# Differential attention of a hybrid layer: a packed stationary block for the sample rows, a shorter softmax merge, and squares on ScalarE

## The reference, cut to what matters

```python
z = h @ w_in                                   # q1|q2, k1|k2, v of a head are 3 x 128 of its columns
q, k = rope_partial(q), rope_partial(k)        # first quarter of each 64-wide half
s = einsum('bqhmd,bkhmd->bhmqk', q, k) * 64**-0.5   # two maps m per head, chunk-causal mask
p = softmax(s)
a = p[:, :, 0] - lam * p[:, :, 1]
attn = a @ v
attn = rms_norm(attn, subln_g) * (1 - lam_init)     # per row and head, over 128 values
```

## Time and profile before

| | |
|---|---|
| median of 3 runs | 946.29 us (943.45 to 947.93) |
| the profiled execution's own time | 945.17 us |
| its span | 943.2 us |
| mean granted TensorE clock | 0.96 of 2.4 GHz |
| busy: PE, PEld, DVE, ACT, POOL | 851.2, 750.7, 603.1, 505.3, 107.6 us |

### The profile page before, as it was taken

One profiled execution on the slowest core, in us unless ns is written; L12 is line 12 of the kernel. 1 busy time (PEld: TensorE's weight loads), 2 busy tenths in 40 slices (PEclk: granted clock), 3 DMA queues, 4 the chain that ended last, 5 costly groups with the idle time before them and its releaser, 6 DMA issues.

```text
span 943.2 us, 15744 instructions
## 1 busy us (share of the span) xinstructions
PE 851.2 (90%) x5052; PEld 750.7 (80%) x5052; DVE 603.1 (64%) x1047; ACT 505.3 (54%) x907; POOL 107.6 (11%) x115
## 2 busy tenths in 40 slices
PE   4998999999999999899899998189999999999980
PEld 4998999888888889889898787167777778777760
DVE  6264224676676676566555311658989998998892
ACT  6235213554544544354623212158878887887883
POOL 0000000000000000000000001202432342233221
PEclk8999999999999999999999998579999999999995
DMA  8622133033033023041322914779999999999975
GB/s 247 153 90 65 51 90 84 14 97 96 0 96 96 24 78 97 9 153 43 112 77 82 353 47 158 234 229 315 330 318 333 343 333 346 345 329 327 342 258 202
DMA packets 156131, 164.99 MB, mean 175 GB/s; under 512 B 20877, under 2 KB 140301, under 8 KB 156090
## 3 DMA queue, kind: packets, MB, share of 16 engines
q1 hardware_dynamic: 149706, 152.69, 49.9%
q0 software_dynamic: 6096, 11.17, 4.4%
q10 hardware_dynamic: 288, 0.59, 0.2%
HBM read 153.71 MB, written 19.60 MB: 184 GB/s over the span
## 4 chain that ended last, share of the span: by engine, by line
PE 74%; DVE 8%; DMA 6%; ACT 5%; issue 4%; SPq 2%; ACTq 0%; POOL 0%; DVEq 0%; POOLq 0%
PE ps L1355 23%; PE ps L1357 21%; PE ps L1356 21%; DMA rawM<-in_w_expert_up 2%; PE ps L1494 2%; ACT E L760 2%; SPq L470 2%; PE ps L1663 1%; PE ps L1503 1%; DMA xg<-h_rows,idn 1%; PE ps L1616 1%; DVE wl L951 1%; PE ps L1475 1%; ACT wh L724 1%; DMA gb<-in_norm_mix_g 1%
## 5 line engine op out<-in xcount | busy, mean ns | idle before, releaser
L1298 DVE TENSOR_TENSOR wl<-rawM,wh 128x1024 fp32r<-128x1024 f32 x192 | 227.3, 1221 | 24.2 <-ACT wh L873 23.8
L873 ACT ACTIVATE wh<-rawM 128x1024 fp32r<-128x1024 f32 x195 | 199.2, 1055 | 12.0 <-PE ps L1357 7.9
L1355 PE MATMUL ps<-hTh,wh 128*128 128x272 f32 x448 | 132.6, 296 | 8.1 <-ACT plh L712 3.0
L1357 PE MATMUL ps<-hTh,wl 128*128 128x272 f32 x448 | 131.2, 293 | 0.0
L1356 PE MATMUL ps<-hTl,wh 128*128 128x272 f32 x448 | 130.4, 291 | 0.0
L1355 PE MATMUL ps<-wh,hTh 128*128 128x384 f32 x320 | 116.4, 364 | 8.4 <-ACT qkv L737 6.8
L1355 PE MATMUL ps<-wh,xh 128*128 128x512 f32 x256 | 105.0, 410 | 4.5 <-DVE xl L1321 3.6
L1357 PE MATMUL ps<-wh,hTl 128*128 128x384 f32 x320 | 108.1, 338 | 0.0
L1356 PE MATMUL ps<-wl,hTh 128*128 128x384 f32 x320 | 107.8, 337 | 0.0
L1357 PE MATMUL ps<-wh,xl 128*128 128x512 f32 x256 | 101.9, 398 | 0.0
L1356 PE MATMUL ps<-wl,xh 128*128 128x512 f32 x256 | 101.8, 398 | 0.0
(11 more groups left out here) (255 smaller groups left out, 1679.7 us busy)
## 6 DMA issues: line engine op xcount, KB each, us to landing
rawM<-in_w_expert_gate SPq DMA_DIRECT2D x131, 256.0 KB, 5.9
rawM<-in_w_expert_up SPq DMA_DIRECT2D x131, 256.0 KB, 8.3
rawM<-in_w_expert_down SPq DMA_DIRECT2D x64, 512.0 KB, 9.1
rawA<-in_w_in SPq DMA_DIRECT2D x64, 192.0 KB, 3.0
rawA<-in_w_in SPq DMA_DIRECT2D x20, 512.0 KB, 5.1
rawA<-in_w_attn_branch SPq DMA_DIRECT2D x8, 512.0 KB, 4.5
rawA<-in_w_out SPq DMA_DIRECT2D x8, 512.0 KB, 4.2
x<-in_x_prompt SPq DMA_DIRECT2D x4, 512.0 KB, 6.8
```

The costliest lines, as they stand in the source:

```text
L873: nc.scalar.activation(wh[:, c % S, :], rawM[:, slot, :], ACT.Copy).then_inc(m_hi, 1)
L1298: V.tensor_tensor(wl[:, c % S, :], rawM[:, slot, :], wh[:, c % S, :].bitcast(F32), ALU.subtract).then_inc(m_lo, 1)
L1355: T.matmul(out, sh, mh_, start=start, stop=False, **kw)
L1357: return T.matmul(out, sl, mh_, start=False, stop=stop, **kw)
```

## The change

It has these parts. (a) The projection of tile 4 takes a stationary block of 128 columns out of a new tile `dec`, which holds for each j the low parts of the 32 sample rows in columns 64 to 95 and their high parts in 96 to 127 of its window; the first 64 columns of the window are the block before, or zeros. Two matmuls (by `wh`, by `wl`) then give the low rows' products in rows 64 to 95 and the high rows' in 96 to 127 of the bank. (b) `join_sample` on VectorE adds rows 64 to 95 to rows 96 to 127 in `qkv`; the next head's tile 4, `rope` and ScalarE's high part of v wait for it. (c) Map one is no longer scaled; map two is scaled by `esum1 * (1/esum2) * (-lambda)` (`ratio`) and added in one pass, and the row's factor 1/`esum1` is applied by the ScalarE copy into `att`. Map one's exponent gets an addend log(2^-9). (d) The clamp is one operation over tiles 0 to 2 and one over tiles 3 and 4 of a head; squares are ScalarE's alone, a head later, out of `clamped`; VectorE's squares and five of the eight last small operations go.

```diff
 # ScalarE
@@ rows_hi
+                if t == 4:
+                    nc.scalar.activation(dec_hi.rearrange("p (b k) n -> p b k n", b=2), v, ACT.Copy)
+            def square(g, t):
+                act.wait_ge(cl_done, 2 * g + (1 if t < 3 else 2))
+                nc.scalar.activation(clamped[:, t, :], clamped[:, t, :], ACT.Square, scale=SQ_SCALE,
+                                     accum_out=ssb[:, t, bass.ds(g, 1)]).then_inc(sq_done, 1)
             def step(g, s):
+                if s < NT and not (isinstance(g, int) and g == 0):
+                    square(g - 1, s)
                 if s >= 2:
                     act.wait_ge(av_mm, NT * g + s - 1)
-                    nc.scalar.activation(bsq[:], ps[:, 7, 0:P], ACT.Square, scale=BIG_SCALE,
-                                         accum_out=ssb[:, s - 2, bass.ds(g, 1)])
-                    nc.scalar.activation(att[:, s - 2, g, :], ps[:, 7, 0:P], ACT.Copy).then_inc(av_ev, 1)
+                    nc.scalar.activation(att[:, s - 2, g, :], ps[:, 7, 0:P], ACT.Copy,
+                                         scale=rinv[:, s % 2, 0:1]).then_inc(av_ev, 1)
@@ attend
                 act.wait_ge(ckv_in, 32 * (g + 1))
+                act.wait_ge(dec_done, g + 1)
@@ after the last head
             step(HEADS - 1, NT)
+            for t in range(3):
+                square(HEADS - 1, t)
             step(HEADS - 1, NT + 1)
             gate_block(5)
+            for t in range(3, NT):
+                square(HEADS - 1, t)
             warm(ACT.Sqrt)
 # VectorE
@@ rows_lo, t == 4
+                    V.tensor_tensor(dec_lo.rearrange("p (b k) n -> p b k n", b=2), v, oh, ALU.subtract)
+            def clamp(g, part, lk):
+                tiles = slice(0, 3) if part == 0 else slice(3, NT)
+                dve.wait_ge(av_ev, NT * g + (3 if part == 0 else NT))
+                dve.wait_ge(sq_done, NT * (g + 1))
+                V.tensor_scalar(clamped[:, tiles, :], att[:, tiles, g, :], CLAMP, -CLAMP, ALU.min,
+                                ALU.max).then_inc(cl_done, 1)
@@ step(g, s, lk, join=None)
                     lk(V.reciprocal(rinv[:, t % 2, :], esum[:, t % 2, :]))
-                    V.tensor_tensor(rinv[:, t % 2, 1:2], rinv[:, t % 2, 1:2], nlam[:], ALU.mult)
                     a0, a1 = E[t % 2][:, 0, 0:n], E[t % 2][:, 1, 0:n]
-                    lk(V.tensor_scalar(a0, a0, rinv[:, t % 2, 0:1], None, ALU.mult))
-                    V.scalar_tensor_tensor(out=a0, in0=a1, scalar=rinv[:, t % 2, 1:2], in1=a0,
+                    lk(V.scalar_tensor_tensor(out=ratio[:, t % 2:t % 2 + 1], in0=esum[:, t % 2, 0:1],
+                                              scalar=rinv[:, t % 2, 1:2], in1=nlam[:], op0=ALU.mult, op1=ALU.mult))
+                    V.scalar_tensor_tensor(out=a0, in0=a1, scalar=ratio[:, t % 2:t % 2 + 1], in1=a0,
                                            op0=ALU.mult, op1=ALU.add).then_inc(am_done, 1)
+                if join is not None:
+                    join_sample(join)
@@ the same step, after atl
-                if s >= 2:
-                    dve.wait_ge(av_ev, NT * g + s - 1)
-                    lk(V.tensor_scalar(asq[:], att[:, s - 2, g, :], CLAMP, -CLAMP, ALU.min, ALU.max))
-                    ins = V.scalar_tensor_tensor(out=asq[:], in0=asq[:], scalar=1.0,
-                                                 in1=asq[:], op0=ALU.mult, op1=ALU.mult,
-                                                 accum_out=ssa[:, s - 2, bass.ds(g, 1)])
-                    lk(ins)
+                if s == NT:
+                    clamp(g, 0, lk)
+            def join_sample(g):
+                dve.wait_ge(acc_ev, NT * (g + 1))
+                V.tensor_tensor(qkv[LAST:P, 4, :], ps[2 * DEC:LAST, 4, 0:384], qkv[LAST:P, 4, :],
+                                ALU.add).then_inc(dec_done, 1)
@@ attend
                 nxt(3)
+                if not (isinstance(g, int) and g == 0):
+                    clamp(g - 1, 1, lk)
                 nxt(4)
@@ head
-                if not first:
-                    step(h - 2, NT, lk)
+                if first:
+                    join_sample(h - 1)
+                else:
+                    step(h - 2, NT, lk, h - 1)
                 rope(h - 1, lk)
-                if not first:
-                    step(h - 2, NT + 1, lk)
 # TensorE, project
                             pe.wait_ge(acc_ev, NT * (h - 1) + t + 1)
+                            if t == 4:
+                                pe.wait_ge(dec_done, h)
+                    if t < 4:
+                        ins = three(ps[:, t, 0:384], hTh[:, j, col(t)], hTl[:, j, col(t)], wh[:, sl, wc], wl[:, sl, wc],
+                                    j == 0, j == KD - 1)
+                    else:
+                        both = dec[:, 2 * DEC * j:2 * DEC * j + P]
+                        T.matmul(ps[:, t, 0:384], both, wh[:, sl, wc], start=j == 0, stop=False)
+                        ins = T.matmul(ps[:, t, 0:384], both, wl[:, sl, wc], start=False, stop=j == KD - 1)
```

More of the change, by code:

```diff
@@ L148, in build @@
         rinv = small("rinv", [P, 2, 2])
-        ssa = small("ssa", [P, NT, HEADS])
         rsa = small("rsa", [P, NT, HEADS])
         ssb = small("ssb", [P, NT, HEADS])
+        shift = small("shift", [P, 2])
+        ratio = small("ratio", [P, 2])
         wgt = small("wgt", [P, NT, 2])
@@ L825, in _ @@
             step(HEADS - 1, NT)
+            for t in range(3):
+                square(HEADS - 1, t)
             step(HEADS - 1, NT + 1)
             gate_block(5)
+            for t in range(3, NT):
+                square(HEADS - 1, t)
             warm(ACT.Sqrt)
             act.wait_ge(ms_done, 1)
-            nc.scalar.activation(rsa[:], rsa[:], ACT.Sqrt).then_inc(rt_done, 1)
+            nc.scalar.activation(rsa[:], rsa[:], ACT.Sqrt, scale=1.0 / P).then_inc(rt_done, 1)
             split_to(AB0 + 1)
@@ L962, in _ @@
             V.memset(U[:, :, 0:BUF], 0.0).then_inc(pad_done, 1)
+            V.memset(shift[:, 0:1], math.log(MAP_SCALE))
+            V.memset(shift[:, 1:2], 0.0)
+            V.memset(dec[:, 0:2 * DEC].bitcast(F32), 0.0)
             V.memset(idi[:, ROWS:ROWS + 2], 0)
@@ L1059, in lo_head, with step @@
                                 ALU.subtract).then_inc(lo_done, 1)
-            per_head = 1 + 6 * NT
-            per_tail = 6
-            def step(g, s, lk):
+            per_head = 1 + 4 * NT
+            per_tail = 2
+            def clamp(g, part, lk):
[4 more added lines that the diff above has]
+                                ALU.max).then_inc(cl_done, 1)
+            def step(g, s, lk, join=None):
                 if 1 <= s <= NT:
@@ L1081, in step @@
                     lk(V.tensor_reduce(mx[:, s % 2, :], ps[:, 5:7, 0:n], AX.X, ALU.max))
-                    V.tensor_scalar(nb[:, s % 2, :], mx[:, s % 2, :], -SCALE, None, ALU.mult).then_inc(nb_done, 1)
+                    V.scalar_tensor_tensor(out=nb[:, s % 2, :], in0=mx[:, s % 2, :], scalar=-SCALE, in1=shift[:],
+                                           op0=ALU.mult, op1=ALU.add).then_inc(nb_done, 1)
                 if 1 <= s <= NT:
@@ L1156, in _ @@
             split[0] = GB0 + 3
-            step(HEADS - 2, NT, link)
+            step(HEADS - 2, NT, link, HEADS - 1)
             rope(HEADS - 1, link)
-            step(HEADS - 2, NT + 1, link)
             attend(HEADS - 1, lambda k: split_to({3: GB0 + 3, 4: GB0 + 5, 5: GB0 + 7, 6: 0}[k]), link)
             step(HEADS - 1, NT, link)
[L1162 to L1171, removed]
-            link(V.tensor_scalar(fin[:], fin[:], -1.0, 1.0, ALU.mult, ALU.add))
-            link(V.tensor_tensor(rsa[:], rsa[:], fin[:], ALU.mult))
-            link(V.tensor_tensor(rsa[:], rsa[:], isb[:], ALU.add))
-            V.tensor_scalar(fin[:], ssb[:], one, 2.0 ** -20, ALU.is_lt, ALU.mult).then_inc(ms_done, 1)
+            clamp(HEADS - 1, 1, link)
+            full = 2.0 ** 128 * SQ_SCALE ** 2
+            dve.wait_ge(sq_done, NT * (HEADS + 1))
+            link(V.tensor_scalar(rsa[:], ssb[:], full, 1.0 / SQ_SCALE, ALU.min, ALU.mult))
+            V.tensor_scalar(fin[:], ssb[:], full, 2.0 ** -20, ALU.is_lt, ALU.mult)
+            V.tensor_scalar(rsa[:], rsa[:], P * EPS * SQ_SCALE, None, ALU.add).then_inc(ms_done, 1)
             dve.wait_ge(rt_done, NT + 1)
```

19 lines of the change are left out of this document (10 added, 9 removed).

## The result

The changed kernel takes 940.05 us (median of 11 executions, 937.55 to 941.95) and the one before 945.56 in the same runs: ratio 0.9939, 95% interval 0.9928 to 0.9951. The forecast was 939.8 us, with a gain of 6.5 us; the medians differ by 5.5. The profiled execution took 940.75 us with a span of 938.9.

The account below looks back on a forecast made before the run. The kernel looks bound by TensorE, but at five waits chains over other engines end last. Priced by segment, the terms sum to -6.5 us, from 946.3 to 939.8 us (own range 937.5 to 942; full range 934.8 to 945).

Parts of the forecast that it names:

- Head 0 and start of head 1: Head 0's projection and head 1 up to `turn`, where TensorE alone counts: -1.4 and -0.35 us.
- Projection to `turn`: Next head's projection start to the transposes of q and k: -0.6 us in each of six heads, -3.6 in all.
- it had 0.28 to wait: Before the transposes of q and k: TensorE saves 0.35, waited 0.28, so could be ready 0.63 us earlier.
- `turn` to scores 0: Transposes of q and k to scores 0: scaled copy into `att` adds 0.05 us, six times, +0.3.
- Scores 0 to 1: VectorE's chain before scores 1: clamp between two low parts of weights adds 0.28 us, seven times, +2.0.
- Scores 1 to scores 2: Segment with no wait of TensorE: one matmul less, -0.18 us, seven times, -1.2.
- scores 2 to map 2: Scores 2 to map 2's transposes: scale pass goes, `ratio` costs some 0.17; -0.28 us, eight times, -2.2.
- The rest of a head: Map 2's transposes to the next projection: 0 gained, bank wait from 1.11 to about 1.3 us; join covered, no cost.
- The gross: Rival: TensorE's waits are slack and all 11.3 us of removed matmuls count, giving 935.0 us; chance 0.12.
- The eaten gain: Rival: added VectorE clamps run at 0.29 us per tile and eat the gain, 942.5 to 945 us; chance 0.24.
- The clock: Rival: longer TensorE waits bring the clock to 0.50 once a head in six heads, +12, 951.8 us; chance 0.03.
- The join: Rival: the join ends 1.5 + 0.7 us later than placed and lengthens a head, 942 to 947 us; chance 0.05.

Follow-up runs that it names:

- e3: The changed kernel with map one scaled in a pass of its own again and att copied without a scale; ratio to before 0.9946, period 33.55 us.
- e4: The kernel before with late squares on ScalarE and grouped clamps only; ratio to before 1.0008, period 34.06 us.
- e5: The changed kernel with the clamp of tiles 3 and 4 moved to after step 0; ratio to before 0.9934, period 33.07 us.
- e1: The changed kernel with tile 4 projected by three matmuls again, without packing and join; ratio to before 0.9985, period 33.80 us.
- e2: The kernel before with packing and join and nothing else; ratio to before 0.9935, periods 33.57 to 33.66 us.
- e9: The changed kernel with e5, e7, e8 and the clamp cut of e6 together; 925.04 us median, ratio to before 0.9787, period 31.82 us.
- e6: The changed kernel with the clamps cut 4 tiles + 1 instead of 3 + 2; single execution of 939.7 us, period 33.23 us.
- e10: The changed kernel with a gap of 8 elements behind each 128 in `clamped`; single execution of 938.3 us, period 33.30 us.
- e7: The changed kernel with ScalarE emptying banks 0 and 1 before the high part of weight part 6; ratio to before 0.9895, period 32.72 us.
- e8: The changed kernel with VectorE's low part of weight part 5 made after step 3, not step 2; ratio to before 0.9875, period 32.52 us.

## Why the prediction was right, step by step

*Head 0 and start of head 1.* Forecast -1.4 - 0.35 = -1.75; from head 0's first matmul to `turn` of head 0 it was 26.30 before and 24.53 after: -1.77. Head 0's projection alone took 19.65 us for 21.06, where 19.6 for 21.0 was forecast.

*Projection to `turn`.* Forecast -0.60, measured -0.50. The step that failed is "it had 0.28 to wait": that is the idle time of the weight loads, which run ahead of the matmuls and so wait longer (before map 2 they wait 0.54 in the kernel before, the matmuls 0.22). The rows could have told: the five waits add up to 2.24 us, but TensorE's matmuls leave only 34.10 - 32.74 = 1.36 of a head idle, nearly all of it the 0.22 and the 1.11. The matmul of `turn` stood 292.48 - 292.18 = 0.30 behind the one before it, where 0.177 is the plain distance, so TensorE lost 0.12; this and the two removed matmuls, 0.35, give the 0.5 measured. The clamp was mis-sized as well (0.35 forecast and 0.30 from start to start; 0.54 and 0.46 measured), and it cost nothing, since `rope` still ended first.

*`turn` to scores 0.* Forecast +0.05 with bounds 0 and +0.15, measured -0.04, outside them. The copy with its scale does take 0.37 us for 0.27, as weighed, but the segment is no longer for it: e3, whose copy has no scale, has 3.98 as the changed kernel has. The gain came with the late squares, for e4 with these alone has 3.97 for 4.02.

*Scores 0 to 1.* Forecast +0.28, measured +0.20: the clamp lasts 0.28 but the next instruction starts 0.20 after its start. e5 takes exactly that away. The weight loads' wait there grew from 0.35 to 0.73, where about 0.8 was forecast.

*Scores 1 to scores 2, scores 2 to map 2.* Forecast -0.18 and -0.28, measured -0.18 and -0.27. e1, e2, e3 and e4 show which part each belongs to. Before map 2 the matmuls waited 0.22; now 0.13 is left (to 272.15 from the end of the one before, 271.68 + 0.34), under 0.3 as forecast. The weight loads wait 0.46 there, but 0.27 in e1, which has the merge and no packing: the packed blocks bring TensorE earlier. So where work of the same engine ahead of a wait gets shorter, the wait that remains says nothing about the segment. The weight loads in the changed kernel, then in e1:

```profile
272.14 0.31 PEld L1541 LDWEIGHTS ps<-cst,E 128*128 128x128 f32 x3 [0.46 <-DVE E L1104]
```
```profile
275.53 0.31 PEld L1518 LDWEIGHTS ps<-cst,E 128*128 128x128 f32 x3 [0.27 <-DVE E L1098]
```

*The rest of a head.* Forecast 0, measured -0.01 and 0; the wait for the bank is 1.3 as forecast, and the join takes 0.56 and ends over 1 us ahead of its use.

*Sum.* From head 0's first matmul to the first one of the output's projection (454.05) it is 323.84 us for 330.99: -7.15, where -6.5 was forecast; a head gave -0.80 for -0.73. That the head comes out so close is in part luck: over the six heads the segment up to `turn` gave 0.6 us less than forecast, while the two that were to get longer cost 1.1 less. What the medians show is 5.5. The forecast of 939.8 lies within 0.3 of the measured 940.05 because its base, 946.3, was 0.7 above the median of the eleven and its gain 1.0 above the 5.5. The stretch behind that matmul was 482.35 us in the profile before and 484.85 in the one after, 2.5 more (and head 0 begins 0.35 later), and this is over the 2 us that the prediction named as its own refutation outside the heads. The ten experiments, whose code there is the same, have 481.75 (e4) to 485.43 (e1) in their profiles, e9 482.33, without relation to what was gained ahead. So I take it for a scatter between executions, not for an effect. The clock is a part of it: 35 executions of the kernel before, run beside the experiments, took 944.0 us on average where the mean granted clock was 0.963 or 0.964 (12 of them) and 947.6 where it was 0.957 or 0.958 (6). And it can be seen in the traces: behind TensorE's wait of 2.81 us in front of that matmul the clock falls to 0.50 (1.2 GHz) in both kernels, but at another moment. Before, then after:

```profile
462.00:465.00 3.00, 3.00 (x16) 3.00 (x16) 1.06 (x1) 2.99 (x6) 0.00 (x0) 0.55 0.61 189
465.00:468.00 3.00, 3.00 (x24) 3.00 (x23) 0.00 (x0) 2.32 (x4) 0.00 (x0) 0.88 0.83 271
```
```profile
452.00:455.00 3.00, 0.95 (x4) 0.95 (x5) 3.00 (x4) 2.98 (x4) 0.00 (x0) 0.72 0.00 0
455.00:458.00 3.00, 3.00 (x15) 3.00 (x15) 1.27 (x2) 2.99 (x6) 0.00 (x0) 0.50 0.50 170
458.00:461.00 3.00, 3.00 (x18) 3.00 (x17) 0.00 (x0) 2.52 (x4) 0.00 (x0) 0.64 0.78 259
```

By the clock's share that is 3 x 0.45 + 3 x 0.12 = 1.7 us lost before and 3 x 0.50 + 3 x 0.36 = 2.6 after; the 0.95 us of matmuls up to 455 ran slow too (the two at 454.67 and 454.90 stand 0.23 apart, where before they stand 0.12 to 0.13 apart until 462), 0.5 more. So the clock explains about 1.4 us. The other 1.1 of the 2.5 stay open. In e2, e4, e5, e6 and e10 the clock stays at 1.00 behind the same wait, and the stretch takes 481.75 to 483.17 us; the five others lose 1.7 us by the same count and take 482.33 to 485.43.

*The rivals.* The gross fell with e1 and e2. The eaten gain fell with the clamps of 0.20 and a covered 0.46. The clock stayed at 1.00 in the heads of every profile; behind head 7's projection it fell in two (e5, e6), for 1.5 us each. The argument against this rival was weak there: a reading at 444 can't show a fall at 388, since the one of e5 was over before 384, within about 5 us of its wait. The clock did read 1.00 from 388 to 397 in the kernel before. The wait behind head 7's projection, which the forecast left at 1.74, grew to 1.89, as the one in the loop did. The join became late only where its cover was taken (e7, and e9 with the same order).

## What to carry to other kernels

Price a removed matmul by the segment between two waits, and read each segment's own last chain; here about 0.5 of the gross 1.42 us a head was left, and moving one VectorE instruction of 0.96 us by a step gave as much as the whole change. Read TensorE's loss from the distance of its matmuls, not from the idle time of its weight loads, and another engine's cost from start to start. When an edit leaves TensorE waiting longer for one engine, look first at that engine's order: e9's moves remove no work and bring about 14.5 us (a ratio of 0.9787 for 0.9939), the change itself 5.5.

## What was not expected of the hardware

A one-operand VectorE pass over three pieces of 128 took 0.54 us where two took 0.28 and four 0.42, and 0.42 with a gap in the destination. After TensorE's wait of 1.9 us behind head 7's projection the clock fell in two profiles (e5, e6) and stayed at 1.00 in five (the changed kernel, e2, e3, e8, e10); a fall cost 1.5 us. After the one of 2.81 us it fell in seven of twelve, both kernels among them, at another moment and for another time.
